# Finishing the two row tiles of an output product apart, and moving the first low weight pieces of the next stage to GpSimd

## What is computed

```
def swiglu(h, w_in, w_out):                      # D_MODEL 1024, D_FF 2816
    a, u = jnp.split(h @ w_in, 2, axis=-1)
    return (jax.nn.silu(a) * u) @ w_out
...
y = swiglu(modulate(x, sh0, sc0), ffn_w_in[i, 0], ffn_w_out[i, 0])
x = post_norm_residual(x, y, g0, FFN_RES, ln_g[i, 0], ln_b[i, 0])   # layer_norm(ALPHA*x + res*(1+gate)*y)
h = modulate(x, sh1, sc1)
y = retention(h, ...)            # or nsa, even_mix, fox_mix, peer_ffn, third mix: all end in  ... @ w_out
x = post_norm_residual(x, y, g1, 1.0, ln_g[i, 1], ln_b[i, 1])
```

## Time and profile before

| | |
|---|---|
| median of 3 runs | 3731.51 us (3731.25 to 3734.38) |
| profiled execution, its own time | 3730.45 us |
| its span in the trace | 3728.6 us, 59526 instructions |
| PE busy | 3587.4 us, 96% |
| DVE busy | 2996.0 us, 80% |
| ACT busy | 2044.1 us, 55% |
| POOL busy | 141.0 us, 4% |

### The profile page before, as it was taken

The page is one execution under the profiler, slowest core; times in us unless marked ns, Lnnn a source line. Parts: engine busy times, 40 slices in busy tenths (PEclk is TensorE's granted clock), DMA queues, the critical chain, the costliest instruction groups (busy, mean ns, idle before and its releaser), DMA issues. The chain is left out here.

```text
span 3728.6 us, 59526 instructions
## 1 busy us (share of the span) xinstructions
PE 3587.4 (96%) x22218; PEld 3071.4 (82%) x22218; DVE 2996.0 (80%) x6294; ACT 2044.1 (55%) x4309; POOL 141.0 (4%) x148
## 2 busy tenths in 40 slices
PE   6999899999999879999999999999999999999898
PEld 5887688888788758998888887899988888887787
DVE  7887588887788776988888956689788897799866
ACT  3554455655455545545666456554566654555555
POOL 0000000000200001300000000050000000000000
PEclk9999999999899979999999999999999999999999
DMA  8767376676367514545555454244455544687454
GB/s 330 275 256 286 113 287 249 265 260 241 118 249 275 185 60 164 179 152 181 181 181 181 169 191 160 106 175 162 170 181 181 181 170 181 229 304 267 152 187 154
DMA packets 119616, 744.49 MB, mean 200 GB/s; under 512 B 13857, under 2 KB 14273, under 8 KB 44833
## 3 DMA queue, kind: packets, MB, share of 16 engines
q1 hardware_dynamic: 118082, 737.57, 53.9%
q10 hardware_dynamic: 416, 2.07, 0.1%
q0 software_dynamic: 832, 1.06, 0.1%
HBM read 738.54 MB, written 1.05 MB: 198 GB/s over the span
## 5 line engine op out<-in xcount | busy, mean ns | idle before, releaser
L230 PE MATMUL bank<-h_split,weights_high 128*128 128x512 f32 (+1 forms) x5824 | 1711.8, 358 | 14.6 <-DVE h_split L748 8.7
L1141 ACT ACTIVATE weights_high<-weight_ring 128x512 fp32r<-128x512 f32 x2248 | 1292.5, 624 | 645.8 <-PE bank L230 390.6
L1149 DVE TENSOR_TENSOR weights_low<-weight_ring,weights_high 128x512 fp32r<-128x512 f32 x2168 | 1395.3, 687 | 294.6 <-ACT weights_high L1141 273.0
L230 PE MATMUL bank<-h_split,weights_low 128*128 128x256 f32 x4800 | 1267.5, 280 | 0.0
L230 PEld LDWEIGHTS bank<-h_split,weights_high 128*128 128x128 f32 x5824 | 1013.1, 189 | 160.8 <-issue 14.6
L230 PEld LDWEIGHTS bank<-h_split,weights_low 128*128 128x128 f32 x4800 | 909.6, 189 | 37.9 <-issue 0.4
L230 PE MATMUL acc<-weights_high,hidden_high 128*128 128x512 f32 x1552 | 612.9, 395 | 2.4 <-DVE hidden_low L1323 2.4
L230 PE MATMUL acc<-weights_low,hidden_high 128*128 128x512 f32 x1552 | 604.8, 390 | 0.0
L230 PE MATMUL acc<-weights_high,hidden_low 128*128 128x512 f32 x1552 | 604.7, 390 | 0.0
L230 PEld LDWEIGHTS acc<-weights_high,hidden_low 128*128 128x128 f32 x1552 | 291.3, 188 | 63.3
L230 PEld LDWEIGHTS acc<-weights_low,hidden_high 128*128 128x128 f32 x1552 | 291.7, 188 | 59.3 <-issue 0.2
(11 more groups left out here) (360 smaller groups left out, 3383.1 us busy)
## 6 DMA issues: line engine op xcount, KB each, us to landing
weight_ring<-stream SPq DMA_DIRECT2D x574, 1024.0 KB, 4.8
h_feat<-slots SPq DMA_DIRECT2D x96, 512.0 KB, 5.7
h_tok<-slots SPq DMA_DIRECT2D x94, 512.0 KB, 5.8
work<-slots SPq DMA_DIRECT2D x26, 512.0 KB, 8.3
mod_sums<-biases SPq DMA_DIRECT2D x7, 1536.0 KB
h_feat<-rows SPq DMA_DIRECT2D x8, 512.0 KB, 3.7
work<-rows SPq DMA_DIRECT2D x7, 512.0 KB, 4.4
work<-biases SPq DMA_DIRECT2D x1, 1536.0 KB
```

The costliest lines, as they stand in the source:

```text
L230: ins = self.nc.tensor.matmul(out, lhs, rhs, start=start, stop=stop)
L1141: act.activation(k.w_hi[:, b, q * self.QUARTER:(q + 1) * self.QUARTER], self.raw(g, q), ACT.Copy).then_inc(k.highs_ready, 1)
L1149: return eng.tensor_tensor(k.w_lo[:, b, w], self.raw(g, q), k.w_hi[:, b, w].bitcast(F32), ALU.subtract)
```

## The change

Three edits.

1. In `TwoLayers` and `OutProj` the last two halves are no longer multiplied one after the other. `out_half` multiplies row tile 0 of the last half but one, then row tile 0 of the last half (and signals `acc_filled`), then row tile 1 of the last half but one, then row tile 1 of the last half. The last half but one is counted in `pending_halves` only behind its row tile 1.
2. For a dense stage behind a boundary that updates `x`, the low pieces of its first two halves are made by GpSimd (`early_low`), in the boundary's list. DVE made those of half 0 in the boundary and those of half 1 as the first thing of the next stage; it makes neither now.
3. PE waits for these on `lows_by_pool` in place of `lows_ready`.

```diff
     def early_lows(self, dve):
-        for g in range(self.next.lows_ahead):
-            self.next.split_low(dve, g)
+        if not self.next.ahead_by_pool:
+            for g in range(self.next.lows_ahead):
+                self.next.split_low(dve, g)
+
+    def gpsimd(self, pool):
+        if self.next is not None and self.next.ahead_by_pool:
+            for g in range(self.next.lows_ahead):
+                self.next.early_low(pool, g)
...
         pool.tensor_copy(self.kept, k.slot(s)[:, 0:self.kept.shape[1]]).then_inc(k.rows_kept, 1)
+        super().gpsimd(pool)
...
             self.products(pe, g, k.w_hi[:, b, :], k.w_lo[:, b, :])
-            k.pending_halves += 1
+            if not (self.staggered and g == self.n - 2):
+                k.pending_halves += 1
         self.tensor_end()
+
+    def out_half(self, pe, c, tile, hi, lo):
+
+        if c == self.chunks - 2:
+            tile(0, c, hi, lo)
+            self.kept = hi, lo
+            return
+        if c < self.chunks - 2:
+            for t in range(TT):
+                tile(t, c, hi, lo)
+            return
+        tile(0, c, hi, lo).then_inc(self.k.acc_filled.sem, 1)
+        tile(1, c - 1, *self.kept)
+        self.k.pending_halves += 1
+        tile(1, c, hi, lo).then_inc(self.k.acc_filled.sem, 1)
...
             if self.gates is None or g != self.gates_after + 1:
                 pe.wait_ge(k.vector_for_tensor.sem, k.vector_for_tensor.take())
-            for t in range(TT):
...
+            self.out_half(pe, c, self.out_tile, hi, lo)
...
+    def out_tile(self, t, c, hi, lo):
+
+        k = self.k
+        x_hi, x_lo = (x[:, c % 2, t * P:(t + 1) * P] for x in (k.g_hi, k.g_lo))
+        for h in range(2):
+            w = slice(h * 512, (h + 1) * 512)
+            for i, (x, a) in enumerate(((x_hi, hi), (x_hi, lo), (x_lo, hi))):
+                end = c == self.chunks - 1 and i == 2
+                mm = k.mm(k.acc[:, 2 * t + h, :], x, a[:, w], start=c == 0 and i == 0, stop=end, last=end and h == 1)
+        return mm
...
         if dense and isinstance(before, KeyScores):
             stage.ahead, stage.lows_ahead, stage.ahead_by_pool = EARLY, EARLY, True
+        elif dense and isinstance(before, Boundary) and before.update is not None:
+            stage.ahead, stage.lows_ahead, stage.ahead_by_pool = EARLY, EARLY, True
         elif dense and isinstance(before, Inputs):
             stage.ahead, stage.lows_ahead = EARLY, 1
```

More of the change, by code:

```diff
@@ L1119, in take_halves @@
         self.follow, self.inputs, self.have = None, None, 0
+        self.staggered = False
     def count_lows(self):
@@ L1245, in __init__ @@
         self.take_halves(len(self.halves))
+        self.staggered = True
         self.gates_after, self.gates = 24, None
@@ L1345, in products, with out_tile @@
             pe.wait_ge(k.input_lows.sem, self.more + (c - DC) // 2 + 1)
[L1346 to L1355, removed]
+        self.out_half(pe, c, self.out_tile, hi, lo)
+    def out_tile(self, t, c, hi, lo):
+        k = self.k
+        y_hi, y_lo = (y[:, c % DC, t * P:(t + 1) * P] for y in (k.h_hi, k.h_lo))
+        for h in range(2):
+            w = slice(h * 512, (h + 1) * 512)
+            for i, (y, a) in enumerate(((y_hi, hi), (y_hi, lo), (y_lo, hi))):
+                end = c == self.chunks - 1 and i == 2
+                mm = k.mm(k.acc[:, 2 * t + h, :], y, a[:, w], start=c == 0 and i == 0, stop=end, last=end and h == 1)
+        return mm
     def next_pair(self, g):
```

## The result

| | before | changed |
|---|---|---|
| median, 17 runs each | 3731.46 us (3729.75 to 3734.38) | 3739.57 us (3734.17 to 3747.33) |
| profiled execution, its own time | 3730.45 us | 3739.80 us |

The ratio is 1.002, 95% interval 1.0013 to 1.0026: 8.1 us slower in the medians, 9.35 in the profiled executions. The forecast was 3743.8 within 3736.5 to 3750.

What follows compares the result with a forecast made beforehand. PE, busy 96% of the span, idles at boundaries behind a DVE, ACT and PE chain that sets the time. Terms 5.9 + 0.85 + 0.25 + 1.1 + 4.2 = +12.3 us gave 3742.8 profiled, median 3743.8, range 3736.5 to 3750.

Steps and rivals of the forecast that it cites:

- rival A: Whole kernel: contention between DVE and GpSimd costs little; +5.9, at most +7, so 3737 to 3739; chance 0.20.
- boundary 10: Boundary 10 keeps its order of tiles and its adds read PSUM: 0.
- PE's wait behind `TwoLayers`: Behind `TwoLayers`, PE waits 1.12 for `hidden_low` at the last half's row tile 0 and ends 1.12 later.
- ACT's late release, boundaries 1, 3, 4, 11: The last half but one is released later, delaying ACT's squares: +3.7 at 1, 3 and 4, +1.5 at 11.
- Boundaries 7 and 9: No idle time in ACT there, so the later release costs 1.36 each, +2.7 together.
- Boundary 2: No table load, so the square comes earlier: -1.2; GpSimd's second piece delays add 1: +0.85.
- the lock: GpSimd and DVE instructions with two SBUF inputs take turns: +0.85 at 2, +0.25 at 5, +1.1 at 12, +4.2 at 6.
- 12: Boundary 12: -0.6 without a table load; GpSimd's pieces among DVE's multiply-adds and adds: +1.1.
- 5: Boundary 5: later release less ACT's idle time, +0.1; GpSimd's last piece ends behind DVE's wish, +0.25.
- Boundary 6: Low pieces gone from DVE: -0.3; GpSimd's four pieces alternate with DVE's centres, add and refresh: +4.2.
- DVE loses four times 1.3: Boundary 6: DVE loses 1.3 to each of GpSimd's four pieces, less about 1 of slack: +4.2.
- Rival C, the clock: Low granted clock for one more step at several boundaries: two or three steps cost 3 to 6 us, 3747 to 3750; chance 0.15.

Runs made afterwards that it cites:

- e1: Edit 1 alone against the kernel before, low pieces left on DVE: 3734.98 us, ratio 1.0015.
- e5: As e1, and in front of gated boundaries ACT makes half 1's high pieces behind root 0: 3741.81 us, ratio 1.0046 to the kernel before.
- e8: As e5, but edit 1 behind `OutProj` only in front of gated boundaries: 3737.86 us, ratio 1.0043 to the kernel before.
- e2: Edits 2 and 3 alone against the kernel before, halves in the old order: 3737.33 us, ratio 1.0017.
- e6: The changed kernel, but the stage behind `Renorm` (boundary 6) keeps its low pieces on DVE: 3738.83 us, ratio 1.0019 to the kernel before.
- e11: The kernel of e6 measured once more: 3739.82 us, ratio 1.0018 to the kernel before.
- e3: Edit 1 behind `TwoLayers` only, low pieces on DVE, against the kernel before: 3738.41 us, ratio 1.0017.
- e4: Edit 1 behind `OutProj` only, low pieces on DVE, against the kernel before: 3732.8 us, ratio 1.0002.
- e12: The kernel of e1 measured once more: 3737.03 us, ratio 1.0012 to the kernel before.
- e9: As e8, but without edit 1 behind `TwoLayers`: 3728.5 us, ratio 0.9994 to the kernel before.

## Why the prediction was right, and what was mis-sized

The side, the places and the mechanisms held; the forecast was 4.2 us too high, and the median of 3739.57 lies in its range but just under its own band of 3740 to 3747, between that and rival A's. The way from +12.3 to +8.1: the forecast's own terms measured 9.0, 3.3 less; boundary 10, which it had at nothing, gave 1.0; the stretches between boundaries gave -0.6; and the median stood 1.01 above the profiled execution before and 0.23 below it after, another -1.2. The last three are no part of the forecast's mechanism, and single executions of one kernel differ by as much.

- **PE's wait behind `TwoLayers`**: forecast 1.12, measured 1.03. `acc` ends 1.05 to 1.23 later at 1, 3, 4, 6 and 13, and 1.36 at 11. Right.
- **ACT's late release, boundaries 1, 3, 4, 11**: forecast 3.7 + 1.5, measured 3.5 + 1.6. e1 has the same without GpSimd, e5 takes most of it away at 1, 3 and 4 by ACT's order alone. Right, though e5 and e8 showed a second path close under it that I had left out: PE's 32 scale matmuls, and behind them DVE's scales and normalise 1.
- **Boundaries 7 and 9**: forecast +1.36 each. The squares are late by exactly that, the next stage by 1.02. Before, the transposes stood behind 13 matmuls of 128x512 on PE that `hold_clock` issues only to keep PE busy (they started at 1416.89, though normalise 0 ended at 1416.43); that slack of some 0.4 took the rest. The term was too large by 0.7 in all.
- **Boundary 2**: forecast -1.2 and +0.85 for the lock; measured -1.40 (e1) and +0.56. **12**: forecast -0.6 and +1.1; measured -0.65 and +0.61. **5**: forecast +0.1 and +0.25; measured +0.06 and +0.01.
- **Boundary 6**: forecast -0.3 and +4.2; measured -0.16 and +3.11. The mis-sized step is "DVE loses four times 1.3": each instruction lost 0.6 to 1.1, not a whole piece of 1.3, and 3.1 in all. The durations fit an instruction that waits only for what is left of the other engine's. The row that the forecast took as its nearest had this size already: in the earlier trace rows four subtractions of 0.41 took 4.72, so they lost 0.77 each, 3.1 in all.
- **The lock itself**: the question that no row of before answered was whether a `SCALAR_TENSOR_TENSOR` contends. It does: 1.93, 2.28, 1.90, 2.09 here, and 1.86 in e2. The Trainium skill, "SBUF — State Buffer", section "Who interferes with whom", says so for VectorE instructions with two SBUF inputs, and this trace agrees. DVE's weighs, which read PSUM, kept 1.22 to 1.23 beside GpSimd, as the earlier trace rows had it.
- **Rival C, the clock**, was partly at work. Boundary 10 has no edit in its chain that costs, yet it lost 1.00: its 32 scale matmuls took 5.15 instead of 4.16. The windows of the changed kernel show why:

```profile
3216.40:3219.00 2.60, 2.58 (x21) 2.59 (x21) 2.19 (x4) 2.36 (x6) 0.75 (x1) 0.90 0.70 296
3219.00:3221.60 2.60, 2.60 (x14) 2.60 (x14) 0.05 (x2) 0.10 (x2) 0.00 (x0) 0.50 0.00 0
```

The same stretch of before, from where its matmuls start:

```profile
3209.00:3211.60 2.60, 2.58 (x23) 2.58 (x24) 2.19 (x4) 2.36 (x6) 0.00 (x0) 1.00 0.70 296
3211.60:3214.20 2.60, 2.60 (x17) 2.60 (x17) 0.65 (x6) 0.32 (x3) 0.00 (x0) 0.61 0.00 0
```

By these shares the low clock (1.2 GHz) began some 2.1 us behind the start of the 32 matmuls in the changed kernel, and some 3.1 us behind it in the kernel before. e6 and e11 are one kernel and have +1.02 and -0.22 there, so it is not the edit by itself. Nor are the values at 12 free of it: e3, which leaves that boundary as it was, has +0.35 there, and e4 and e8 have +0.68 and +0.59 where e1, with the same order, has -0.65. In 15 us around it the mean granted clock is 0.77 in e3, e4 and e8 and 0.89 in e1 and before. Single values of the table at 10, 11 and 12 can carry over a microsecond of clock. The spread of the changed kernel, 13 us against 5 of before (8 over its 111 executions), may be of that kind: its executions with the lowest mean clock (0.979) took 3741.47 and 3747.33.
- **Rival A** (3737 to 3739, the lock costs little) was nearer to the medians than the forecast's middle: the pooled total is +7.4 (6.4 to 8.5). Its reason doesn't hold, though. Edit 1 alone costs 4.8 (3.4 to 6.3) and GpSimd alone, in e2, 7.1 (4.8 to 9.5). Each hides part of the other, and so GpSimd adds only 2.6 to edit 1, and edit 1 only 0.4 (-2.3 to 2.8) to GpSimd.

## What to carry to other kernels

An early result helps only if every engine on the chain can follow: here row tile 0 was ready 0 to 1.4 us earlier, and the buffer that the same reordering released 1.4 to 2.8 us later held another engine's in-order list, in which the wanted work stood last. Before reordering matmuls, list what each one releases and what stands behind the instruction that waits for it. In this kernel GpSimd as a helper for VectorE was free only where VectorE idled or read PSUM; in the chain of operations with two SBUF inputs each piece cost VectorE 0.6 to 1.1 us, so a piece of 0.69 saved there is no gain.

## What was not expected of the hardware

- In 4 of e5's 12 executions and 3 of e8's 12 the time was some 40 us longer than in the others (3774 to 3781 us; beside them one of e8 took 13.9 ms and one of e3 15.2 ms, of which there is no trace), and in none of the 28 of the changed kernel, the 22 of e1 and e12, or the 11 of e9. e5's profile is one of them. Its windows show the granted clock at half from about 937 to 1032, inside a stage that no edit touches, with PE busy for all of 60 us of it:

```profile
900.00:930.00 30.00, 29.02 (x164) 25.05 (x164) 20.30 (x35) 13.36 (x26) 0.00 (x0) 1.00 0.55 217
930.00:960.00 30.00, 29.00 (x139) 22.80 (x137) 13.85 (x69) 12.84 (x32) 2.70 (x5) 0.61 0.26 71
960.00:990.00 30.00, 30.00 (x146) 25.73 (x144) 12.34 (x64) 10.66 (x28) 0.00 (x0) 0.50 0.00 1
990.00:1020.00 30.00, 30.00 (x131) 24.74 (x132) 12.30 (x50) 8.53 (x19) 4.34 (x6) 0.50 0.00 1
```

Its boundary 5 came 40.9 us later than before's, measured from boundary 4. The profiled execution of e8, not one of its long ones, has 0.94 in the second of these windows and 0.94 in the third. PE was busy for 29.00 us of the second in both. What decides between the two I can't say from these traces. A median hides such executions where they are few; the list of single times showed them.
- Equal instructions in equal order gave single executions of 3734 to 3747 us. With one trace for each kernel, only sums over places that the edit touches could be compared; totals needed over 20 executions to tell 2 us.
